# Feed-forward up product: every second tile pair as seven quarter products of 256 columns

## The chip, the cores and the metric

The kernel runs on one core of a Trainium2 chip. The metric is the time of one execution on the device in microseconds (us); shown are the median of the runs and, for a profiled execution, its own time.

## What is computed

The reference runs two blocks over 512 tokens of width 1024, in float32. The change touches one product of the first:

```python
h = _rmsnorm(x, g_pre_ffn[i])
u = _causal_dwconv(h @ w_up[i], w_conv[i], b_conv[i])
a, v = u[..., :D_FF], u[..., D_FF:]
x = x + _rmsnorm((jax.nn.gelu(a) * v) @ w_down[i], g_post_ffn[i])
```

`w_up` is 1024 x 5632: 22 gate tiles of 128 output features and 22 value tiles. The convolution is causal, of width 3, along the tokens.

## The kernel before

Instructions are written by hand for each engine, in the order in which that engine runs them; semaphores order the engines. Each float32 matrix of the large products is split in two of the rounded type fp32r, a high part (a rounded copy) and a low part (the rest), and a product is the sum of three: high weights by high x, high weights by low x, low weights by high x.

In the up product (the stage, 418 to 657.6 us) the weights are the stationary operand and x, transposed, the moving one: `hT_r` is its high part, `up_low` its low part, 8 blocks of 128 features by 512 tokens. For every tile `split_features` (L423) gives 16 matmuls at L431 as soon as the high part of the tile is there, and 8 at L434 when the low part is: 24 matmuls of 512 columns, and 48 for a pair of gate tile and value tile. The sums of a pair stand in two of the eight PSUM banks, `2 * (j % 4) + w`, so four pairs are in flight.

The other engines, for tile n of pair j:
- SP loads the 512 KB tile into one of 12 ring slots (L2102), up to 12 tiles ahead; the slot is free once PE has used the tile in it.
- ACT makes the high part (`high_act`, L379), one tile ahead and into one of two places, once PE has used the tile before the last; then it takes the finished tile through the last tap of the convolution with its bias (L2763), and once a pair applies gelu (L2770).
- POOL makes the low part (`low_pool`, L394), a subtraction of 1024 columns.
- DVE adds the other two taps from PSUM (L3065, L3067) and multiplies gate and value into `gT` (L3071). At the last pair it also splits the first two row tiles of the down product (L420, L421).

Other lines that the rows name: L456, a product with the tokens stationary, 416 and 280 columns wide, same type; L1165, a product in float32; L421 and L2719, other splits; L2311, the transposed x going to SBUF ahead of the stage; L1256, expert weights; L724, L3085 and L2970, other elementwise work. The down product (L476) follows the stage.

## Time and profile before

| | us |
|---|---|
| median of 3 runs | 1539.93 (1539.74 to 1540.53) |
| profiled execution, its own time | 1538.59 |
| its span | 1536.8 |
| the stage, pairs 0 to 21 | 418 to 657.6 |
| share of the span: PE, DVE, ACT, POOL busy | 97%, 43%, 33%, 33% |

The span runs from the first to the last instruction on record; 1.8 us lie around it. A busy PE share of 97% says that TensorE almost always had a matmul in it, and not that every matmul was needed. Matmuls overlap, so what one costs is the distance of two starts.

### The profile page before, as it was taken

Reading aid. Unit: us, or ns where it says so; the run is one execution under the profiler, and the core shown is the slowest. Engines: PE = TensorE matmul, PEld = TensorE weight load, DVE = VectorE, ACT = ScalarE, POOL = GpSimd, SP = SyncE. Lnnn points to the kernel's source line nnn. Section 1 sums busy time; section 2 is a strip of 40 time slices with the busy share of each in tenths; the row PEclk is TensorE's granted clock in tenths of the full one; section 3 lists DMA queues with packets and bytes.
Section 4 is the critical chain, followed back from the end, with each engine's and each line's share of the span. In section 5 each row is a group of like instructions: output and inputs, shape, how many; then the busy total and the mean of one; then the engine's idle time right before and its main releaser. Section 6 shows DMA issues by size and latency. Waiting matters only on the chain.

```text
span 1536.8 us, 19531 instructions
## 1 busy us (share of the span) xinstructions
PE 1495.9 (97%) x7629; PEld 1019.5 (66%) x7630; DVE 667.6 (43%) x1141; ACT 508.5 (33%) x917; POOL 513.6 (33%) x328
## 2 busy tenths in 40 slices
PE   8999999999999999999999999999999999999997
PEld 7976677888788888888888777468543443433433
DVE  4157664224733333423335778664533232332334
ACT  4246664223533333321246333424111111111112
POOL 3454664445344444444724362622100010010000
PEclk9999999999999999999999999999999999999999
DMA  8233002322322222232323222267999999999996
GB/s 313 98 109 95 1 2 97 98 100 99 115 96 96 96 96 96 97 97 99 97 92 122 91 82 69 109 256 289 361 429 428 431 418 430 429 429 421 424 426 252
DMA packets 52636, 306.87 MB, mean 200 GB/s; under 512 B 7098, under 2 KB 7354, under 8 KB 40001
## 3 DMA queue, kind: packets, MB, share of 16 engines
q1 hardware_dynamic: 47872, 292.03, 49.2%
q0 software_dynamic: 4096, 11.49, 2.0%
q10 hardware_dynamic: 576, 2.10, 0.3%
q8 instruction: 63, 1.03, 0.3%
q14 instruction: 29, 0.23, 0.1%
HBM read 303.39 MB, written 4.19 MB: 200 GB/s over the span
## 4 chain that ended last, share of the span: by engine, by line
PE 86%; DMA 6%; DVE 5%; ACT 1%; POOL 1%; issue 1%; SPq 0%; DVEq 0%; ACTq 0%
PE banks L431 19%; PE banks L1256 13%; PE banks L476 12%; PE banks L434 9%; DMA ring<-experts 6%; PE banks L1302 5%; PE banks L1311 3%; PE banks L1056 2%; PE banks L456 2%; PE banks L2484 2%; PE banks L2468 2%; PE banks L2550 1%; PE banks L2454 1%; PE banks L914 1%; PE banks L915 1%; PE banks L2443 1%
## 5 line engine op out<-in xcount | busy, mean ns | idle before, releaser
L394 POOL TENSOR_TENSOR arena_r<-ring,arena_r 128x1024 fp32r<-128x1024 f32 x143 | 353.2, 2475 | 414.1 <-ACT arena_r L379 394.5
L379 ACT ACTIVATE arena_r<-ring 128x1024 fp32r<-128x1024 f32 x143 | 150.5, 1058 | 441.4 <-PE banks L434 279.4
L431 PE MATMUL banks<-hT_r,arena_r 128*128 128x512 f32 x640 | 250.0, 391 | 0.0
L431 PE MATMUL banks<-arena_r 128*128 128x512 f32 x640 | 249.1, 389 | 0.0
L1256 PE MATMUL banks<-ring,arena 128*64 128x512 f32 x704 | 222.5, 605 | 12.0 <-DMA ring<-experts 12.0
L476 PE MATMUL banks<-arena_r 128*128 128x512 f32 x784 | 183.5, 389 | 0.6 <-DVE arena_r L421 0.6
L476 PEld LDWEIGHTS banks<-arena_r 128*128 128x128 f32 x784 | 147.1, 188 | 31.5 <-POOL arena_r L394 1.0
L1256 PEld LDWEIGHTS banks<-ring,arena 128*64 128x64 f32 x704 | 70.5, 139 | 142.4 <-issue 141.5
L431 PEld LDWEIGHTS banks<-hT_r,arena_r 128*128 128x128 f32 x640 | 120.1, 188 | 29.0 <-issue 3.4
L431 PEld LDWEIGHTS banks<-arena_r 128*128 128x128 f32 x640 | 120.2, 188 | 25.1 <-issue 0.2
L751 POOL MEMSET arena<- 128x1024 f32 x15 | 14.3, 952 | 341.8 <-PE banks L1209 332.8
L434 PE MATMUL banks<-hT_r,arena_r 128*128 128x512 f32 x520 | 128.4, 389 | 0.0
L1949 DVE TENSOR_TENSOR resid<-resid,banks 128x1024 f32<-128x1024 f32 x60 | 70.6, 1218 | 127.2 <-PE banks L1311 127.2
L1302 PE MATMUL banks<-arena 128*64 128x512 f32 x496 | 113.6, 595 | 2.5 <-DMA arena<-experts 2.2
L1256 PE MATMUL banks<-arena 128*64 128x512 f32 x278 | 115.9, 595 | 0.0
L434 PEld LDWEIGHTS banks<-hT_r,arena_r 128*128 128x128 f32 x520 | 97.6, 188 | 20.3
L3065 DVE SCALAR_TENSOR_TENSOR arena<-banks,colt,arena 128x511 f32<-128x511 f32 x44 | 33.0, 750 | 151.8 <-ACT arena L2763 151.8
L1302 PEld LDWEIGHTS banks<-arena 128*64 128x64 f32 x496 | 36.5, 137 | 66.3 <-issue 60.5
L1311 PE MATMUL banks<-arena_r,colt_r 128*128 128x512 f32 x256 | 67.5, 404 | 0.1
L1518 ACT ACTIVATE arena<-banks 128x512 f32<-128x512 f32 x16 | 9.6, 597 | 165.6 <-PE banks L1268 165.6
L1311 PEld LDWEIGHTS banks<-arena_r,colt_r 128*128 128x128 f32 x256 | 45.5, 188 | 23.4 <-issue 14.6
L1938 DVE SCALAR_TENSOR_TENSOR arena_r<-banks,colt,arena_r 128x512 fp32r<-128x512 f32 x32 | 24.0, 751 | 82.2 <-ACT arena_r L1548 82.2
(506 smaller groups left out, 2171.6 us busy)
## 6 DMA issues: line engine op xcount, KB each, us to landing
ring<-stream SPq DMA_DIRECT2D x164, 512.0 KB, 3.3
arena<-experts SPq DMA_DIRECT2D x35, 2048.0 KB, 15.6
ring<-experts SPq DMA_DIRECT2D x32, 2048.0 KB, 16.6
ring<-experts SPq DMA_DIRECT2D x17, 1024.0 KB, 17.3
arena<-experts SPq DMA_DIRECT2D x31, 512.0 KB, 10.1
arena<-experts SPq DMA_DIRECT2D x11, 1024.0 KB, 15.9
ring<-experts SPq DMA_DIRECT2D x14, 512.0 KB, 6.4
hT<-experts SPq DMA_DIRECT2D x8, 512.0 KB, 11.0
```

What stands on the lines that cost most here:

```text
L379: nc.scalar.activation(parts(name, m)[:, 0, :], tile(tile_n), ACT.Copy).then_inc(S["w_high"], 1)
L394: nc.gpsimd.tensor_tensor(w[:, 1, :], tile(tile_n), plain(w[:, 0, :]), ALU.subtract).then_inc(S["w_low"], 1)
L431: nc.tensor.matmul(pb[:, bank, :], w[:, 0, k * P:(k + 1) * P], b[:, k, :], start=(k == 0 and part == 0), stop=False)
L434: last = nc.tensor.matmul(pb[:, bank, :], w[:, 1, k * P:(k + 1) * P], high[:, k, :], start=False, stop=(k == ND - 1))
L456: last = nc.tensor.matmul(pb[:, bank0 + i, 0:width], a[:, k, i * P:(i + 1) * P], w[:, v, q * width:(q + 1) * width], start=(k == 0 and par ...
L476: last = nc.tensor.matmul(pb[:, 2 * i + h, :], u[row], w[:, v, h * 512:(h + 1) * 512], start=(k == 0 and row + v == 0), stop=(k == K - 1 a ...
L1056: last = nc.tensor.matmul(pb[:, 2 * i + h, :], rows[row][:, i * P:(i + 1) * P], w[:, v, h * 512:(h + 1) * 512], start=(k == 0 and part == ...
L1256: last = nc.tensor.matmul(pb[r, bank, :], XT[:, k, r], weights(b, c + e, k * 512, (k + 1) * 512), start=(k == 0), stop=(k == ND - 1))
L1302: last = nc.tensor.matmul(pb[r, 3 + h, :], hbT[:, k, r], weights(b, 4 + e, at, at + 512), start=(k == 0), stop=(k == 3))
L1311: last = nc.tensor.matmul(pb[:, bank, :], spread_r[:, i * P:(i + 1) * P], y[:, h * 512:(h + 1) * 512], start=(part == 0), stop=(part == 1 ...
L1949: TT(half, half, pb[:, first:second + 1:second - first, :], ALU.add).then_inc(S["added"], 1)
L3065: L(nc.vector.scalar_tensor_tensor(out=c[:, 1:T], in0=u[:, 0:T - 1], scalar=col("w_conv", 2 * NF + m), in1=c[:, 1:T], op0=ALU.mult, op1=AL ...
```

## The change

Pairs 2, 4, ... 20 (ten, `MIXED`) are computed in another way, the twelve others as before. Take the pair's weights as 2 x 2 blocks, gate and value by the two halves of the 1024 features, and x as 2 x 2 blocks, the two halves of the features by the two halves of the tokens. Eight quarter products (128 outputs, 512 features, 256 tokens) make the pair; the change makes seven from sums of the blocks (Winograd's form) and joins them by additions:

- PE: `up_term`, seven products of 12 matmuls of 256 columns, 84 in place of 48 of 512. Term q writes half a bank of banks 4 to 7; plain pairs use banks 0 to 3, two in flight.
- DVE, once ahead of the stage's work: 4 sums `hT_r + up_low` of x quarters, t1 to t4 from them, and their low parts (`x_low`), all of 1024 columns. For each changed pair: `weight_sums`, 4 operations of 512 columns in SBUF, and `join`, 7 of 256 columns with a PSUM operand.
- ACT: the high parts of t1 to t4, and for each changed pair 7 copies of 512 columns (`term_high`) in place of 2 of 1024, and a copy of the first product (`take_first`). Their order is s3, s4, value_2, gate_1, gate_2, s2, s1 (`TERM_ORDER`), while PE takes gate_1 first.
- POOL: 7 subtractions of 512 columns in place of 2 of 1024, in the same order.
- SP: the t parts lie in eight of the twelve ring slots until the stage ends, so tiles from pair 2 on use four. A load now waits until the tile two pairs back is split. Eight of the down tiles are loaded at the stage's end.
- Some semaphores are shared under a new name (`gate_sig`, `branch_hi`, `branch_lo`), with counts to match.

```diff
+MIXED = range(2, NF, 2)
+PLAIN = [j for j in range(NF) if j not in MIXED]
+LIVE = 4
...
+TERMS = ["gate_1 x_1", "gate_2 x_2", "s2 t2", "s1 t1", "s3 t3", "s4 x_4", "value_2 t4"]
+TERM_ORDER = [4, 5, 6, 0, 1, 2, 3]
+NQ = len(TERMS)
...
+PLACES_OF = [(0, 0), (0, 1), (1, 0), (1, 1), (2, 0), (2, 1), (3, 0)]
...
+        quads = [(slice(4 * k, 4 * k + 4), slice(256 * t, 256 * t + 256)) for k in range(2) for t in range(2)]
+        h_quads = [x_sums[:, 4096 + 1024 * q:5120 + 1024 * q].rearrange("p (k t) -> p k t", k=4) for q in range(4)]
+        t_whole = {t: x_sums[:, 1024 * q:1024 * q + 1024].rearrange("p (k t) -> p k t", k=4) for q, t in enumerate(("t1", "t2", "t3", "t4"))}
+        t_parts = {t: [ring_r[:, spare_slots[at + v], :].rearrange("p (k t) -> p k t", k=4) for v in range(2)]
+                   for t, at in (("t1", 4), ("t2", 6), ("t3", 0), ("t4", 2))}
+        x_parts = [[part[:, k, tok] for part in (hT_r, up_low)] for k, tok in quads]
+        t_parts.update({"x_1": x_parts[0], "x_2": x_parts[2], "x_4": x_parts[3]})
+        term_home = [ar_r(2048, 1024), ar_r(3072, 1024), ar_r(0, 1024), ar_r(1024, 1024), ar_r(22528, 1024), ar_r(23552, 1024),
...
+            elif name == "up" and m // 2 - 1 in MIXED:
+                act.wait_ge(S["up_part"], terms_done(m // 2 - 1, 3 if m % 2 else 1))
...
+                before = max(other for other in range(n) if slot(other) == slot(n))
+                if n >= W_UP + 4 + LIVE and W_UP <= before < W_DOWN and slot(n) in live_slots:
+                    sp.wait_ge(S["w_low"], split_at(before - before % 2 + 1))
+                else:
+                    sp.wait_ge(S["w_used"], emptied_at(n))
...
-            low_pool(pool, "up", 2)
+            for j in range(1, NF):
+                if j in PLAIN:
+                    low_pool(pool, "up", 2 * j, 2 * j + 2)
+                    continue
+                for q in TERM_ORDER:
+                    high, low = term_parts[q][:, 0, :], term_parts[q][:, 1, :]
+                    pool.wait_ge(S["w_high"], term_made(j, q))
+                    nc.gpsimd.tensor_tensor(low, term_source(j, q), plain(high), ALU.subtract).then_inc(S["w_low"], 1)
...
+            def up_term(j, q):
+
+                weight, (high, low) = term_parts[q], t_parts[TERMS[q].split()[1]]
+                pe.wait_ge(S["w_high"], term_made(j, q))
+                for k in range(4):
+                    for part, src in enumerate((high, low)):
+                        nc.tensor.matmul(term_bank(j, q), weight[:, 0, k * P:(k + 1) * P], src[:, k, :], start=(k == 0 and part == 0), stop=False)
+                pe.wait_ge(S["w_low"], term_made(j, q))
+                for k in range(4):
+                    last = nc.tensor.matmul(term_bank(j, q), weight[:, 1, k * P:(k + 1) * P], high[:, k, :], start=False, stop=(k == 3))
+                return last
+
             for j in range(NF):
-                if j >= 4:
-
-                    pe.wait_ge(S["up_dve"], 2 * (j - 3))
-                for w in range(2):
-                    split_features(pe, "up", 2 * j + w, 2 * (j % 4) + w, hT_r, up_low, 2)
+                if j in PLAIN:
+                    if j >= 2:
+                        pe.wait_ge(S["up_dve"], 2 * PLAIN[PLAIN.index(j) - 2] + 2)
+                    for w in range(2):
+                        split_features(pe, "up", 2 * j + w, 2 * (PLAIN.index(j) % 2) + w, hT_r, up_low, 2)
+                    continue
+                if j > 2:
+                    pe.wait_ge(S["up_dve"], 2 * (j - 2) + 2)
+                for q in range(NQ - 1):
+                    if TERMS[q].split()[1] in ("t1", "t2", "t3"):
+                        pe.wait_ge(S["up_sums"], summed(TERMS[q].split()[1], "low"))
+                    up_term(j, q).then_inc(S["up_part"], 1)
+                pe.wait_ge(S["up_sums"], summed("t4", "low"))
+                up_term(j, NQ - 1).then_inc(used, 2)
...
+            def term_high(j, q):
+                if q < 4:
+                    act.wait_ge(S["w_used"], W_UP + 2 * (j - 1) + (1 if q < 2 else 2))
+                elif j == 2:
+                    act.wait_ge(S["w_used"], W_UP)
+                elif q < NQ - 1:
+                    act.wait_ge(S["up_part"], terms_done(j - 2, q))
+                else:
+                    act.wait_ge(S["w_used"], W_UP + 2 * (j - 2) + 2)
+                name = TERMS[q].split()[0]
+                if name in SUMS:
+                    act.wait_ge(S["up_sums"], summed(j, name))
+                else:
+                    arrived(act, W_UP + 2 * j + (name == "value_2"))
+                nc.scalar.activation(term_parts[q][:, 0, :], term_source(j, q), ACT.Copy).then_inc(S["w_high"], 1)
...
+            high_act(act, "up", 2)
+            conv_last(0, 0)
+            x_high("t1")
+            x_high("t2")
+            high_act(act, "up", 3)
+            conv_last(0, 1)
+            act.wait_ge(S["w_low"], made(W_UP + 1))
+            x_high("t3")
+            act.wait_ge(S["w_low"], made(W_UP + 3))
+            x_high("t4")
+            gelu(0)
+            for q in TERM_ORDER[:5]:
+                term_high(2, q)
+            conv_last(1, 0)
+            for j in MIXED:
+                for q in TERM_ORDER[5:]:
+                    term_high(j, q)
+                conv_last(j - 1, 1)
+                gelu(j - 1)
+                take_first(j)
+                for w in range(2):
+                    high_act(act, "up", 2 * j + 2 + w)
                 for w in range(2):
                     conv_last(j, w)
-                act.wait_ge(S["up_dve"], 2 * j + 1)
-                nc.scalar.activation(ga[:, j % 2, :], cva[:, j % 2, 0, :], ACT.Gelu_apprx_tanh).then_inc(S["up_gelu"], 1)
+                gelu(j)
+                if j + 2 in MIXED:
+                    for q in TERM_ORDER[:5]:
+                        term_high(j + 2, q)
+                else:
+                    high_act(act, "down", 0)
+                conv_last(j + 1, 0)
...
+            for q, (k, tok) in enumerate(quads):
+                ins = nc.vector.tensor_tensor(h_quads[q], plain(hT_r[:, k, tok]), plain(up_low[:, k, tok]), ALU.add)
+            L(ins)
+            nc.vector.tensor_tensor(t_whole["t1"], h_quads[1], h_quads[0], ALU.subtract).then_inc(summing, 1)
+            nc.vector.tensor_tensor(t_whole["t3"], h_quads[3], h_quads[1], ALU.subtract).then_inc(summing, 1)
+            dve.wait_ge(summing, summed("t1", "whole"))
+            nc.vector.tensor_tensor(t_whole["t2"], h_quads[3], t_whole["t1"], ALU.subtract).then_inc(summing, 1)
+            dve.wait_ge(summing, summed("t2", "whole"))
+            nc.vector.tensor_tensor(t_whole["t4"], h_quads[2], t_whole["t2"], ALU.subtract).then_inc(summing, 1)
+
+            def weight_sums(j):
+                gate_tile, value_tile = tile(W_UP + 2 * j), tile(W_UP + 2 * j + 1)
+                first, second = slice(0, 512), slice(512, 1024)
+                arrived(dve, W_UP + 2 * j)
+                arrived(dve, W_UP + 2 * j + 1)
+                if j > 2:
+                    dve.wait_ge(S["w_low"], term_made(j - 2, TERM_ORDER[-1]))
+                nc.vector.tensor_tensor(s_home["s1"], value_tile[:, first], value_tile[:, second], ALU.add).then_inc(summing, 1)
+                dve.wait_ge(summing, summed(j, "s1"))
+                nc.vector.tensor_tensor(s_home["s2"], s_home["s1"], gate_tile[:, first], ALU.subtract).then_inc(summing, 1)
+                nc.vector.tensor_tensor(value_tile[:, first], gate_tile[:, first], value_tile[:, first], ALU.subtract).then_inc(summing, 1)
+                dve.wait_ge(summing, summed(j, "s2"))
+                nc.vector.tensor_tensor(s_home["s4"], gate_tile[:, second], s_home["s2"], ALU.subtract).then_inc(summing, 1)
...
+                q, other, to = {"c11": (1, first_term, pb[:, 4, 0:256]), "u2": (2, first_term, second_sum),
+                                "u4": (3, second_sum, fourth_sum), "u3": (4, second_sum, third_sum), "c12": (5, fourth_sum, pb[:, 4, 256:512]),
+                                "c22": (3, third_sum, pb[:, 5, 256:512]), "c21": (6, third_sum, pb[:, 5, 0:256])}[what]
...
+            conv(0, 0)
+            x_low("t1")
+            x_low("t2")
+            weight_sums(2)
+            x_low("t3")
+            conv(0, 1)
+            gated_rows(0)
+            x_low("t4")
+            conv(1, 0)
+            for j in MIXED:
+                conv(j - 1, 1)
+                gated_rows(j - 1)
+                for what in ("c11", "u2", "u4", "u3", "c12", "c22", "c21"):
+                    join(j, what)
+                for w in range(2):
+                    conv(j, w)
+                gated_rows(j)
+                if j + 2 in MIXED:
+                    weight_sums(j + 2)
+                else:
+                    dve.wait_ge(S["up_g"], 2)
+                    dve.wait_ge(S["w_low"], term_made(j, TERM_ORDER[-1]))
+                    split_dve(dve, chain, "down", gT, 0, 2)
+                conv(j + 1, 0)
```

DVE, from the transposed x to the first gated product, before (`colt` holds the convolution's weights, `banks` is PSUM):

```order
L2311 SCALAR_TENSOR_TENSOR arena_r<-banks,colt,hT_r 128x512 [waits copied_act] x8
L3065 SCALAR_TENSOR_TENSOR arena<-banks,colt,arena 128x511 [waits up_conv]
L3067 SCALAR_TENSOR_TENSOR arena<-banks,colt,arena 128x510 [waits dve_chain]
L3065 SCALAR_TENSOR_TENSOR arena<-banks,colt,arena 128x511 [waits up_conv]
L3067 SCALAR_TENSOR_TENSOR arena<-banks,colt,arena 128x510 [waits dve_chain]
L3071 TENSOR_TENSOR arena<-arena 128x512 [waits up_gelu,up_dve]
```

From the same point in the changed kernel (`x_sums` holds the x quarters and t1 to t4, `ring` their parts and the loaded tiles):

```order
L2425 SCALAR_TENSOR_TENSOR arena_r<-banks,colt,hT_r 128x512 [waits copied_act] x8
L3253 TENSOR_TENSOR x_sums<-hT_r,arena_r 128x1024 [waits hT_low]
L3253 TENSOR_TENSOR x_sums<-hT_r,arena_r 128x1024 x3
L3255 TENSOR_TENSOR x_sums<-x_sums 128x1024 [waits dve_chain]
L3256 TENSOR_TENSOR x_sums<-x_sums 128x1024
L3258 TENSOR_TENSOR x_sums<-x_sums 128x1024 [waits up_sums]
L3260 TENSOR_TENSOR x_sums<-x_sums 128x1024 [waits up_sums]
L3286 SCALAR_TENSOR_TENSOR arena<-banks,colt,arena 128x511 [waits up_conv]
L3288 SCALAR_TENSOR_TENSOR arena<-banks,colt,arena 128x510 [waits dve_chain]
L3279 TENSOR_TENSOR ring_r<-x_sums,ring_r 128x1024 [waits h_high] x2
L3269 TENSOR_TENSOR arena<-ring 128x512 [waits w_landed5,w_landed4]
L3271 TENSOR_TENSOR arena<-arena,ring 128x512 [waits up_sums]
```

Eight sums now stand ahead of the first convolution, and two low parts and the weight sums of pair 2 ahead of the second.

DVE in the changed kernel from the last join of pair 2 to the sums of pair 4:

```order
L3310 TENSOR_TENSOR banks<-junk,banks 128x256 [waits up_sums,w_used]
L3286 SCALAR_TENSOR_TENSOR arena<-banks,colt,arena 128x511 [waits up_conv]
L3288 SCALAR_TENSOR_TENSOR arena<-banks,colt,arena 128x510 [waits dve_chain]
L3286 SCALAR_TENSOR_TENSOR arena<-banks,colt,arena 128x511 [waits up_conv]
L3288 SCALAR_TENSOR_TENSOR arena<-banks,colt,arena 128x510 [waits dve_chain]
L3294 TENSOR_TENSOR arena<-arena 128x512 [waits up_gelu,up_dve]
L3269 TENSOR_TENSOR arena<-ring 128x512 [waits w_low,w_landed5,w_landed4]
L3271 TENSOR_TENSOR arena<-arena,ring 128x512 [waits up_sums]
L3272 TENSOR_TENSOR ring<-ring 128x512
L3274 TENSOR_TENSOR arena<-ring,arena 128x512 [waits up_sums]
```

The weight sums of a pair stand behind the joins, convolutions and gated product of the changed pair before it.

ACT in the changed kernel over the first pairs:

```order
L482 ACTIVATE arena_r<-ring 128x1024 [waits w_used,w_landed10]
L2899 ACTIVATE arena<-banks,colt 128x512 [waits w_used]
L2908 ACTIVATE ring_r<-x_sums 128x1024 [waits up_sums] x2
L482 ACTIVATE arena_r<-ring 128x1024 [waits w_used,w_landed11]
L2899 ACTIVATE arena<-banks,colt 128x512 [waits w_used]
L2908 ACTIVATE ring_r<-x_sums 128x1024 [waits up_sums,w_low] x2
L2904 ACT_TABLE_LOAD
L2904 ACTIVATE arena<-arena 128x512 [waits up_dve]
L2924 ACTIVATE arena_r<-ring 128x512 [waits up_sums,w_used]
L2924 ACTIVATE arena_r<-arena 128x512 [waits up_sums,w_used]
L2924 ACTIVATE fifth_home_r<-ring 128x512 [waits w_landed5,w_used]
L2924 ACTIVATE arena_r<-ring 128x512 [waits w_landed4,w_used] x2
```

The high part of tile 3 (the second row of L482) now stands behind the copies of t1 and t2, and the five first copies for pair 2 behind the gelu of pair 0. Before, it was L379, L2763, L379, L2763, gelu.

## Rows read from the trace of the kernel before

**Rows 1.** The page: span, busy time by engine, one DMA issue (count, KB, us).
```profile
span 1536.8 us, 19531 instructions
...
PE 1495.9 (97%) x7629; PEld 1019.5 (66%) x7630; DVE 667.6 (43%) x1141; ACT 508.5 (33%) x917; POOL 513.6 (33%) x328
...
ring<-stream SPq DMA_DIRECT2D x164, 512.0 KB, 3.3
```
**Rows 2.** Busy time by stretch: us, PE, PEld, DVE, ACT, POOL, clock, DMA.
```profile
440.00:657.60 217.60, 217.60 (x961) 180.18 (x961) 77.32 (x104) 79.44 (x100) 96.14 (x40) 1.00 0.29 97
```
**Rows 3.** The chain in order of time: start us, us, what.
```profile
423.67 3.63 PE banks L431 x16
427.30 1.81 PE banks L434 x8
```
**Rows 4.** PE in order of time: the third pair's first matmul.
```profile
439.83 0.39 PE L431 MATMUL banks<-hT_r,arena_r 128*128 128x512 f32 x1
```
**Rows 5.** Line 456 alone, by stretch: us, PE, PEld, clock, DMA.
```profile
57.10:75.15 18.05, 18.05 (x96) 17.93 (x96) 1.00 0.36 117
75.15:87.50 12.35, 12.35 (x97) 12.27 (x96) 1.00 0.38 128
```
**Rows 6.** PEld in order of time, the shortest full loads.
```profile
1075.65 2.98 PEld L1165 LDWEIGHTS banks<-arena,resid 128*128 128x128 f32 x26 [0.15 <-DVE arena L1872]
```
**Rows 7.** Groups by line and shape: busy us, mean ns, idle before.
```profile
L394 POOL TENSOR_TENSOR arena_r<-ring,arena_r 128x1024 fp32r<-128x1024 f32 x143 | 353.2, 2475 | 414.1 <-ACT arena_r L379 394.5 <-DVE arena L1699 19.2
...
L724 POOL TENSOR_TENSOR arena<-arena 128x512 f32<-128x512 f32 x4 | 5.1, 1272 | 0.0
...
L379 ACT ACTIVATE arena_r<-ring 128x1024 fp32r<-128x1024 f32 x143 | 150.5, 1058 | 441.4 <-PE banks L434 279.4 <-PE banks L476 99.6 <-PE banks L2555 24.8
...
L2719 ACT ACTIVATE arena_r<-hT 128x512 fp32r<-128x512 f32 x8 | 4.4, 616 | 0.0
...
L2763 ACT ACTIVATE arena<-banks,colt 128x512 f32<-128x512 f32 x44 | 33.5, 761 | 0.0
...
L3085 DVE TENSOR_TENSOR arena<-arena 128x1024 f32<-128x1024 f32 x3 | 3.7, 1225 | 2.6 <-ACT arena L2791 2.6
...
L3065 DVE SCALAR_TENSOR_TENSOR arena<-banks,colt,arena 128x511 f32<-128x511 f32 x44 | 33.0, 750 | 151.8 <-ACT arena L2763 151.8
...
L2970 DVE COPY arena<-banks 128x256 f32<-128x256 f32 x12 | 4.9, 408 | 1.1 <-PE banks L2468 1.1
```
**Rows 8.** DVE and POOL in order of time, where both subtract.
```profile
378.06 13.72 DVE L421 TENSOR_TENSOR arena_r<-arena,arena_r 128x512 fp32r<-128x512 f32 x5 [2.90 <-ACT arena_r L410]
...
377.59 16.45 POOL L394 TENSOR_TENSOR arena_r<-ring,arena_r 128x1024 fp32r<-128x1024 f32 x6 [4.29 <-ACT arena_r L379]
...
647.95 2.41 POOL L394 TENSOR_TENSOR arena_r<-ring,arena_r 128x1024 fp32r<-128x1024 f32 x1 [3.04 <-ACT arena_r L379]
...
650.14 0.77 DVE L3071 TENSOR_TENSOR arena<-arena 128x512 f32<-128x512 f32 x1
```
**Rows 9.** In order of time, before and in the first pairs.
```profile
417.71 4.69 DVE L2311 SCALAR_TENSOR_TENSOR arena_r<-banks,colt,hT_r 128x512 fp32r<-128x512 f32 x7
...
432.98 0.69 DVE L3071 TENSOR_TENSOR arena<-arena 128x512 f32<-128x512 f32 x1 [0.48 <-ACT arena L2770]
...
424.91 2.39 POOL L394 TENSOR_TENSOR arena_r<-ring,arena_r 128x1024 fp32r<-128x1024 f32 x1 [10.26 <-ACT arena_r L379]
...
430.95 1.28 ACT L2770 ACT_TABLE_LOAD   x1
```
**Rows 10.** PE in order of time, two restarts after an idle stretch.
```profile
249.56 0.50 PE L442 MATMUL banks<-arena_r 128*128 128x512 f32 x1 [0.54 <-DVE hT_r L3029]
...
1190.36 1.11 PE L1256 MATMUL banks<-ring,arena 128*64 128x512 f32 x2 [3.23 <-DMA ring<-experts]
```
**Rows 11.** Busy time by stretch around the second restart, columns as in 2.
```profile
1188.00:1192.00 4.00, 1.64 (x4) 0.61 (x6) 0.64 (x1) 0.00 (x0) 0.00 (x0) 0.80 1.02 434
1192.00:1196.00 4.00, 4.00 (x18) 1.58 (x16) 0.00 (x0) 0.00 (x0) 0.00 (x0) 0.77 0.99 422
```

More of the change, by code:

```diff
@@ L89, with loads_before, emptied_at @@
          "inverse": (21, 8, W_IDFT, 2)}
+MIXED = range(2, NF, 2)
+PLAIN = [j for j in range(NF) if j not in MIXED]
+LIVE = 4
 def slot(n):
+    if W_UP + 4 <= n < W_DOWN:
+        return (W_DOWN + (n - W_DOWN) % LIVE - W_OUT2) % RING
     return (n - W_OUT2) % RING
+def loads_before(n):
+    return sum(slot(other) == slot(n) for other in range(n))
+def emptied_at(n):
+    before = max(other for other in range(n) if slot(other) == slot(n))
+    if n >= W_DOWN + LIVE and before < W_DOWN:
+        return W_DOWN
+    return before + 1
 def landings(s):
@@ L2771, in _ @@
+            high_act(act, "down", 1)
+            conv_last(NF - 1, 1)
+            gelu(NF - 1)
             nc.scalar.activation(st[:, 449:450], cs("eps"), ACT.Sqrt)
```

185 lines of the change are left out of this document (129 added, 56 removed).

## The prediction

> **What bounds the kernel now.** The page comes first: a span of 1536.8 us, TensorE busy for 1495.9 of them, no other engine above 43% [rows 1]. Then the stage of the change, by stretch: from the third pair on, 440.0 to 657.6, PE is busy for all of its 217.6 us at full granted clock, while DVE, ACT and POOL work 77, 79 and 96 us of it [rows 2]. The chain in order of time says what a tile costs: 16 matmuls in 3.63 us and 8 in 1.81, so 5.44 us for 24 of 512 columns, **226.7 ns each** [rows 3]. That is the distance between starts; the 389 ns printed beside one matmul [rows 4] includes its way through the array and must not be summed. A pair is 10.88 us. The stage is bound by matmul issue and by nothing else: a saved matmul is saved time, if the other three engines keep up with what replaces it.
>
> **What PE saves.** In ten pairs (2, 4, ... 20) 48 matmuls of 512 columns (10.88 us) become 84 of 256: seven products of 12. The price of one is not in this trace: no product of that shape (128 by 128 weights, rounded type, 256 columns, a load for each) stands in it. The nearest are line 456's, in the same type: 416 columns, 18.05 us for 96, 188.0 ns; 280 columns, 12.35 us for 96, 128.6 ns [rows 5]. The slope, 0.437 ns a column, gives 118 ns at 256; the overhead seen at 512 (226.7 less 512 columns at 2.4 GHz, 13.4) gives 120. I take **119 ns**, since 280 is only 24 columns away. Upper bound: 128.6, if the distance doesn't fall any further because the weight loads set it. Lower bound: 26 loads of 128 by 128 follow each other in 2.98 us, (2.98 - 0.19) / 25 = 112 ns [rows 6]. At 119 a changed pair takes 84 x 0.119 = 10.00 us and saves 0.88; ten save **8.9 us** (0.8 at 128.6, 14.7 at 112).
>
> The Trainium skill has another price. Its page "TensorE: Matmul & The Clock Gate", section "Back-to-back issue gap", gives columns / 2.4 + 2.5 ns, so 109 ns here, and 216 at 512, where this trace has 226.7. By the page alone ten pairs would save 10 x (48 x 0.2158 - 84 x 0.1092) = 12 us. I go by the rows.
>
> **What the others gain in work, steady state.** Durations [rows 7]: POOL subtraction 1.27 us for 512 columns (2.40 for 1024), ACT copy 0.62 (1.06), ACT's convolution step 0.76, DVE step 0.75, DVE over 1024 SBUF columns 1.22, over 256 of PSUM 0.41; over 512 of SBUF 0.69 [rows 9]. Per two pairs (20.9 us): POOL 7 x 1.27 + 2 x 2.40 = 13.7; DVE 4 weight sums, 7 joins, 8 steps, 2 products, 13; ACT 7 short and 2 long copies, 4 convolution steps, 2 gelu and the saved quarter, about 11. All fit. What decides is one chain that now closes a loop. The weight sums of pair j+2 stand on DVE behind the joins, the convolution and the gated product of pair j, because DVE works in order; and PE's first product of j+2 needs four ACT copies and four POOL subtractions, though only the fourth is its own (order s3, s4, value_2, gate_1). Let E be the end of pair j on PE. Last join done E + 0.6; two convolutions on DVE, 4 x 0.78, to E + 3.6; gated product to 4.3; s1, s2, s3 to 6.3; ACT's copy of s3 to 6.9; POOL, 3 x 1.23 + 1.27, to **E + 12.0**. (1.23 apart, an estimate: the next one begins a little before the end of the last, as on DVE, where seven steps of 0.75 take 4.69 [rows 9].) PE needs it at E + 10.88 (the plain pair) + 8 x 0.119 = **E + 11.83**. That is a stall of 0.3 us with semaphores, and a restart after a stall costs 0.1: the first matmul after one lasts 0.50 instead of 0.39 [rows 10]. Nine pairs at 0.4: **3.6 us**. The later products don't wait: POOL delivers every 1.23 us, PE takes 1.43.
>
> **The entry into pair 2.** PE reaches it at 439.83 [rows 4]. DVE gets free at 417.71 + 4.69 = 422.4 [rows 9] and then has, in order: 4 sums of x quarters and 4 t sums of 1024 columns (8 x 1.15, with the same overlap), one convolution (1.55), two low parts (2.3), s1 to s3 (2.0). That is 15.0 us, to 437.4, even undisturbed. But DVE and POOL get in each other's way. Where both subtract in SBUF, five DVE operations of 0.69 us took 13.72 us, while six of POOL's took 16.45, 2.74 each [rows 8]: each waits for the other's whole operation. The smaller pair of rows shows one collision: POOL ends at 650.36, and the DVE product begun at 650.14 ends 0.55 later [rows 8]. DVE steps with a PSUM operand keep 750 ns [rows 7]. So the subtraction of tile 2, at 424.9 before [rows 9], holds up the fourth x sum by 2.1 us, and that of tile 3 the low part of t1 by 1.8. s3 is ready at 422.4 + 19.0 = 441.4. Four ACT copies later, 443.8, PE may start: **4.1 us late**. Its second half needs four POOL subtractions, which begin at 442.2 and meet on DVE the low part of t3 (to 443.2), the first gated product and the low part of t4 (1.1 us more): ready at 449.4 where PE would go on at 445.0, **4.5 us more**. Together 8.6 us, and nothing gives them back, since the stage is bound by PE. ACT is no help: the copy of tile 3 stands in its queue behind the copies of t1 and t2, and the table load of 1.28 us [rows 9] behind the t copies.
>
> **The clock.** PE stood idle for 3.23 us before 1190.36 [rows 10], and the next two stretches of 4 us have a granted clock of 0.80 and 0.77 [rows 11]: part of them at 1.2 instead of 2.4 GHz, (0.20 + 0.23) x 4 = 1.7 us of full-speed work lost. Two idle stretches of 4.1 and 4.5 us with 1 us of work between should do the same once where PE is working: **1.7 us** (0 to 3.4).
>
> **What costs nothing.** In the stage only four ring slots are live; a load waits for the split of the tile two pairs back, some 9 us before its own sums, and lands in 3.3 [rows 1]. After the stage eight down tiles are loaded at once, with four there, 4 x 5.44 us of cover. The last pair is plain, as before, so the passage into the down product is the same. The queue of SP holds nothing else there. The renamed semaphores do nothing.
>
> **Sum.** -8.9 + 8.6 + 3.6 + 1.7 = **+5.0 us**. The profiled execution's own time is 1538.59, so 1543.6; the median of the runs shown is 1539.93, 1.3 above it, so **1544.9 us**.
>
> **Rivals.**
> - *Pair 2 is entered almost in time; faster.* If DVE and POOL share better than [rows 8], the entry costs 2.7 us (undisturbed sum above, ACT and POOL behind it), with no fall of the clock. -8.9 + 2.7 + 3.6 = -2.6: **1537.3**. It decides from 3 us of entry stall downwards. Against it: both durations in [rows 8]. For it: the subtractions seen there are all of 1024 columns, and most of POOL's in the entry are of 512.
> - *The matmul is shorter, 112 ns* [rows 6]. It saves 5.8 more, but PE then reaches each second half earlier (8 x 0.007) and waits for it longer, so some 5.3 of it remain: -0.3, **1539.6**. The 109 ns of the Trainium skill (same page and section) points this way; the 226.7 ns of this trace at 512 columns do not.
> - *The loop is slower*: 0.1 us more at each of the six hand-overs between engines makes 1 us a pair in place of 0.4: +10.4, **1550.3**. For it: one chain runs through PE, DVE, ACT, DVE, ACT and POOL with no slack left, so whatever I left out lengthens it.
> - *The matmul stays at 128.6 ns* [rows 5]: 8.1 less saved, and stalls 0.08 us a pair smaller: +12.4, **1552.3**.
>
> **How the numbers follow.** No change and the edit can be told apart beyond about 0.2%, 3.1 us, so below 1536.8 is faster and above 1543.0 slower. Chances: forecast 0.45, entry in time 0.18, shorter matmul 0.12, slower loop 0.17, longer matmul 0.08. The forecast's own width, 2 us either way, puts a fifth of it within 0.2%; the entry in time is above 1536.8 half the time; the shorter matmul lies mostly inside; the last two are slower. Faster 0.18, same 0.27, slower 0.55. The range goes from the entry in time with a slightly better matmul, 1535.5, to the slower loop and most of the longer matmul, 1551.5.
>
> **What would show it.** Right: starts of the new matmuls 119 ns apart; PE idle before the third pair for about 4 us at 440, waiting for ACT, and 4.5 us inside its first product, waiting for POOL; DVE sums of 2 to 3 us instead of 1.2 between 425 and 448; a granted clock below 1.0 there and nowhere else in the stage; 0.3 to 0.5 us idle before the fifth, seventh ... pair's first low product, ended by POOL. Wrong: matmuls at 112 or 128 ns, an idle of under 3 us at the third pair, or stalls that wait for a load or for DVE's joins.

## The result: 0.24% slower, and the profile after

The changed kernel takes 1544.53 us (median of 10 runs, 1541.54 to 1546.76) beside 1540.3 for the kernel before: ratio 1.0024, 95% interval 1.0015 to 1.0034, or 3.7 us slower (2.3 to 5.2). Executed again (experiment 10, with its own runs of the kernel before beside it) it took 1546.22, ratio 1.0040 (1.0027 to 1.0053), or 6.2 us slower (4.2 to 8.2). The page of the first profile, in which `split_features` is now at L534 and L537, the quarter products at L2692 (high weights) and L2695 (low weights):

```profile
span 1542.2 us, 20400 instructions
...
PE 1495.0 (97%) x7989; PEld 1031.8 (67%) x7990; DVE 746.6 (48%) x1263; ACT 537.1 (35%) x981; POOL 560.5 (36%) x378
...
PE 76%; DVE 10%; DMA 7%; POOL 4%; ACT 2%; issue 1%; SPq 0%; ACTq 0%; DVEq 0%
```

The last line gives the shares of the chain that ended last. In the kernel before it was:

```profile
PE 86%; DMA 6%; DVE 5%; ACT 1%; POOL 1%; issue 1%; SPq 0%; DVEq 0%; ACTq 0%
```

PE's busy time over the whole kernel is the same as before [rows 1], though 8 us of matmuls are gone. In the stage it is 2.0 us less (237.65 against 239.66): part of the matmuls ran at half the clock, and the length printed for the last one before a wait covers some of the wait. Ahead of the stage it is 1.6 us more, at a lower granted clock near 110 us (last section). More of the chain passes through DVE and POOL than before. By stretch (columns as in [rows 2]), the entry into pair 2 and what follows:

```profile
440.00:444.00 4.00, 2.74 (x13) 1.93 (x11) 3.97 (x6) 2.77 (x4) 0.00 (x0) 1.00 0.00 0
444.00:448.00 4.00, 2.00 (x8) 1.78 (x8) 3.93 (x5) 4.00 (x8) 3.62 (x3) 0.70 0.00 0
448.00:452.00 4.00, 0.45 (x2) 0.37 (x2) 3.96 (x5) 0.91 (x3) 4.00 (x3) 0.50 0.00 0
452.00:456.00 4.00, 4.00 (x21) 4.00 (x21) 2.61 (x4) 1.12 (x3) 3.74 (x3) 0.52 0.00 0
456.00:460.00 4.00, 4.00 (x36) 4.00 (x35) 1.20 (x3) 1.84 (x2) 2.64 (x2) 1.00 0.72 266
```

From 444 to 452 PE is busy for 2.45 of 8 us, while DVE hardly stops, and PE's granted clock falls from 2.4 to 1.2 GHz (0.70, then 0.50); from 452 to 456 PE works without a break, still at half the clock. PE in order of time, there and in pair 4:

```profile
440.76 1.98 PE L537 MATMUL banks<-hT_r,arena_r 128*128 128x512 f32 x8
446.00 0.58 PE L2692 MATMUL banks<-hT_r,arena_r 128*128 128x256 f32 x1 [3.26 <-ACT arena_r L2924]
...
447.66 0.41 PE L2692 MATMUL banks<-arena_r 128*128 128x256 f32 x1
451.63 1.22 PE L2695 MATMUL banks<-hT_r,arena_r 128*128 128x256 f32 x4 [3.55 <-POOL arena_r L2283]
...
474.42 0.28 PE L2692 MATMUL banks<-arena_r 128*128 128x256 f32 x1
474.76 0.74 PE L2695 MATMUL banks<-hT_r,arena_r 128*128 128x256 f32 x4
...
476.78 1.12 PE L2692 MATMUL banks<-ring_r,arena_r 128*128 128x256 f32 x8
477.74 0.64 PE L2695 MATMUL banks<-ring_r,arena_r 128*128 128x256 f32 x4
478.22 1.12 PE L2692 MATMUL banks<-ring_r,arena_r 128*128 128x256 f32 x8
```

The last three lines give the price: 8 matmuls from 476.78 to 477.74, 4 to 478.22, **120 ns each**. Before the first low product of pair 4 the distance is 474.76 - 474.42 = 0.34 us instead of 0.12. The chain in order of time names its cause, four POOL subtractions in a row behind one ACT copy:

```profile
468.93 0.64 ACT arena_r L2924
469.58 0.07 issue
469.64 2.55 POOL arena_r L2283 x2
472.20 1.25 POOL fifth_home_r L2283
473.45 1.26 POOL arena_r L2283
```

Why pair 2 was late is seen on DVE and POOL in order of time (L3253: x sums; L3279: low parts of t1 to t4; L3272: s3; L3294: gated product):

```profile
424.55 6.83 DVE L3253 TENSOR_TENSOR x_sums<-hT_r,arena_r 128x1024 f32<-128x1024 f32 x4
431.42 1.23 DVE L3255 TENSOR_TENSOR x_sums<-x_sums 128x1024 f32<-128x1024 f32 x1
...
437.53 4.12 DVE L3279 TENSOR_TENSOR ring_r<-x_sums,ring_r 128x1024 fp32r<-128x1024 f32 x2
...
442.90 0.68 DVE L3272 TENSOR_TENSOR ring<-ring 128x512 f32<-128x512 f32 x1
...
446.80 1.45 DVE L3294 TENSOR_TENSOR arena<-arena 128x512 f32<-128x512 f32 x1
448.17 2.28 DVE L3279 TENSOR_TENSOR ring_r<-x_sums,ring_r 128x1024 fp32r<-128x1024 f32 x1
```

```profile
427.04 3.26 POOL L497 TENSOR_TENSOR arena_r<-ring,arena_r 128x1024 fp32r<-128x1024 f32 x1 [10.26 <-ACT arena_r L482]
437.03 2.41 POOL L497 TENSOR_TENSOR arena_r<-ring,arena_r 128x1024 fp32r<-128x1024 f32 x1 [6.73 <-ACT arena_r L482]
444.38 2.07 POOL L2283 TENSOR_TENSOR arena_r<-ring,arena_r 128x512 fp32r<-128x512 f32 x1 [4.95 <-ACT arena_r L2924]
446.42 1.28 POOL L2283 TENSOR_TENSOR arena_r<-arena,arena_r 128x512 fp32r<-128x512 f32 x1
447.66 1.71 POOL L2283 TENSOR_TENSOR fifth_home_r<-ring,fifth_home_r 128x512 fp32r<-128x512 f32 x1
```

Four x sums take 6.83 instead of some 4.7 us while POOL splits tile 2; two low parts take 4.12 instead of 2.35 beside tile 3. POOL's own operations grow too, 2.07 and 1.71 instead of 1.27. This is the mutual blocking of [rows 8]. ACT was not what held up the start: it stood idle for 1.20 us, waiting for s3, before its first copy for pair 2.

**Where the time is.** The profiles are compared by the starts of PE's matmuls. This profile enters the stage 2.12 us later than before's, with the same instructions ahead of it (experiment 8 and the last section show that the kernel before does so as well), so the stage is compared by itself: 5.7 us longer, from its first to its last matmul. Pair 2 starts 4.06 us late and takes 16.67 us instead of the 10.08 of 84 matmuls; the nine later changed pairs take 10.39 each, the plain ones 10.91. The stage's 5.7 us lie above the interval of the time (2.3 to 5.2), those of experiment 10, 6.0, inside its own; the last section comes back to this.

### The profile page after: what moved, and what is told of

The parts are those of the page before. It is cut to its first block, busy times and chain, and to the rows that moved or that the text cites. A ratio compares the mean times of both kernels' runs of the same rounds, so it can differ in the third digit from the quotient of the medians.

```text
span 1542.2 us, 20400 instructions
## 1 busy us (share of the span) xinstructions
PE 1495.0 (97%) x7989; PEld 1031.8 (67%) x7990; DVE 746.6 (48%) x1263; ACT 537.1 (35%) x981; POOL 560.5 (36%) x378
## 4 chain that ended last, share of the span: by engine, by line
PE 76%; DVE 10%; DMA 7%; POOL 4%; ACT 2%; issue 1%; SPq 0%; ACTq 0%; DVEq 0%
PE banks L1359 13%; PE banks L579 12%; PE banks L534 9%; DMA ring<-experts 7%; PE banks L1405 5%; PE banks L537 5%; PE banks L2692 4%; POOL arena_r L2283 3%; PE banks L1414 3%; PE banks L2695 2%; PE banks L559 2%; PE banks L2598 2%; PE banks L1159 2%; PE banks L2582 2%; PE banks L2664 1%; PE banks L2568 1%
## 5 line engine op out<-in xcount | busy, mean ns | idle before, releaser
L497 POOL TENSOR_TENSOR arena_r<-ring,arena_r 128x1024 fp32r<-128x1024 f32 x123 | 309.7, 2526 | 300.5 <-ACT arena_r L482 281.1
L482 ACT ACTIVATE arena_r<-ring 128x1024 fp32r<-128x1024 f32 x123 | 129.2, 1058 | 317.3 <-PE banks L537 138.3
L534 PE MATMUL banks<-hT_r,arena_r 128*128 128x512 f32 x480 | 188.0, 392 | 0.3 <-ACT arena_r L482 0.3
L534 PE MATMUL banks<-arena_r 128*128 128x512 f32 x480 | 187.0, 390 | 0.0
L579 PE MATMUL banks<-arena_r 128*128 128x512 f32 x784 | 183.5, 389 | 0.6 <-DVE arena_r L524 0.6
L579 PEld LDWEIGHTS banks<-arena_r 128*128 128x128 f32 x784 | 147.1, 188 | 31.5 <-POOL arena_r L497 1.0
L534 PEld LDWEIGHTS banks<-hT_r,arena_r 128*128 128x128 f32 x480 | 90.1, 188 | 23.2 <-issue 3.4
L534 PEld LDWEIGHTS banks<-arena_r 128*128 128x128 f32 x480 | 90.2, 188 | 18.6 <-issue 0.2
L537 PE MATMUL banks<-hT_r,arena_r 128*128 128x512 f32 x360 | 88.9, 389 | 0.0
L537 PEld LDWEIGHTS banks<-hT_r,arena_r 128*128 128x128 f32 x360 | 67.6, 188 | 14.0
L2283 POOL TENSOR_TENSOR arena_r<-ring,arena_r 128x512 fp32r<-128x512 f32 x30 | 40.2, 1353 | 70.8 <-ACT arena_r L2924 70.8
```

The costliest lines, as they stand in the source:

```text
L482: nc.scalar.activation(parts(name, m)[:, 0, :], tile(tile_n), ACT.Copy).then_inc(S["w_high"], 1)
L497: nc.gpsimd.tensor_tensor(w[:, 1, :], tile(tile_n), plain(w[:, 0, :]), ALU.subtract).then_inc(S["w_low"], 1)
L534: nc.tensor.matmul(pb[:, bank, :], w[:, 0, k * P:(k + 1) * P], b[:, k, :], start=(k == 0 and part == 0), stop=False)
L537: last = nc.tensor.matmul(pb[:, bank, :], w[:, 1, k * P:(k + 1) * P], high[:, k, :], start=False, stop=(k == ND - 1))
L579: last = nc.tensor.matmul(pb[:, 2 * i + h, :], u[row], w[:, v, h * 512:(h + 1) * 512], start=(k == 0 and row + v == 0), stop=(k == K - 1 a ...
L2283: nc.gpsimd.tensor_tensor(low, term_source(j, q), plain(high), ALU.subtract).then_inc(S["w_low"], 1)
```

## The experiments

Each is the changed kernel with one edit, unless it says otherwise. The second column is the time against the kernel before as executed beside it, from the ratio and its interval; the third the stage in the profile, against before's 239.6 us.

| | time, us (95%) | stage, us |
|---|---|---|
| changed kernel | +3.7 (2.3 to 5.2) | +5.7 |
| 1 price on PE alone | -9.4 (-11.6 to -7.4) | -7.8 |
| 2 gate_1 split first | +0.5 (-0.8 to 1.8) | +2.7 |
| 3 filler in the waits | +4.6 (3.2 to 6.0) | +3.9 |
| 4 POOL shortened, tiles 2, 3 | +0.8 (-0.5 to 2.2) | +2.3 |
| 5 first changed pair is 4 | -1.1 (-2.5 to 0.3) | -0.5 |
| 6 terms without sums ahead | -4.2 (-5.9 to -2.5) | -2.5 |
| 7 both, and banks | -6.2 (-8.3 to -4.2) | -5.3 |
| 9 weight sums first | +2.8 (1.2 to 4.3) | +2.7 |
| 10 changed kernel again | +6.2 (4.2 to 8.2) | +6.0 |
| 11 filler again | +4.8 (2.9 to 6.5) | +4.0 |

**1, the price of the matmuls.** In the kernel before, for pairs 2, 4, ... 20:

```diff
+                    for i in range(28):
+                        half, k, part = i % 2, i // 4, i // 2 % 2
+                        nc.tensor.matmul(pb[:, bank, 256 * half:256 * half + 256], weight[:, 0, k * P:(k + 1) * P],
+                                         (hT_r, up_low)[part][:, k, 256 * half:256 * half + 256], start=(i == 0), stop=False)
```

and 14 more on the low part.

> The kernel before, in which PE alone is changed: in pairs 2, 4, ... 20 it issues 84 matmuls of 256 columns (42 a tile, 28 on the high part and 14 on the low part) in place of 48 of 512. The last quarter of the sums of those pairs is left out; the other engines do what they did. Theory: the price is the distance of two starts seen in the changed kernel, 0.120 us, so a pair takes 10.08 instead of 10.88 and the whole saving reaches the end: 10 x 0.80 = 8.0 us, about 1532.3 against 1540.3. Rival 1: something else in the stage (ACT's copy, a ring slot, a load) takes the place of PE as the bound and gives part of it back: 0 to -5 us, with waits of PE inside the short pairs. Rival 2: the distance is shorter when two neighbours share their weights, down to 0.109: -17 us at most.

Measured: 1528.65 us, ratio 0.9939. The chain of the first changed pair:

```profile
439.96 3.35 PE banks L2585 x28
443.31 1.68 PE banks L2590 x14
444.99 3.36 PE banks L2585 x28
448.35 1.68 PE banks L2590 x14
450.03 3.65 PE banks L431 x16
```

3.35 / 28 and 1.68 / 14 are 120 ns, though four in a row use the same weights; the pair takes 10.07 us and waits for nothing. The stage is 7.8 us shorter, 8.0 expected. The median fell by more, 11.6 us (9.4 by the ratio, whose interval holds the 8.0). The stage bears out the theory, and both rivals fall: PE waits nowhere in the short pairs, and the distance is not below 120 ns. The gain of the matmuls alone is 8 us, and the changed kernel gives back 13.5 (5.7 + 7.8 in the stage).

**2, the order of the terms.**

```diff
-TERM_ORDER = [4, 5, 6, 0, 1, 2, 3]
+TERM_ORDER = [0, 1, 4, 5, 6, 2, 3]
```

> The changed kernel with one line edited: ACT and POOL split the terms in the order gate_1, gate_2, s3, s4, value_2, s2, s1, so that what PE needs first comes first and does not stand behind the weight sums. Theory (the stall in each later pair is POOL's fourth place behind DVE's sums): the nine gaps of about 0.25 us before the first low product vanish, -2.0 to -2.4; in pair 2 the first two products start almost in time, and the long wait moves to the third product (s2): its first half about 0.8 us late, its second half 4 to 5 us, again for POOL. Together 1.5 to 2 us less there. In all 4.3 us below the changed kernel, about 1540.0. Rival (the loop is set by the sums themselves, wherever the copies stand): gaps of 0.2 us or more reappear before s2's or s3's low product in every changed pair, and the time stays within 1 us of the changed kernel.

Measured: 1540.02 us, ratio 1.0003. All nine later pairs take 10.07 us with no gap, so the rival falls. In pair 2 the wait moved to the third product, as expected:

```profile
445.56 1.18 PE L2692 MATMUL banks<-ring_r,arena_r 128*128 128x256 f32 x8 [0.64 <-ACT arena_r L2924]
451.53 1.22 PE L2695 MATMUL banks<-ring_r,arena_r 128*128 128x256 f32 x4 [4.78 <-POOL arena_r L2283]
```

The stage lost 3.0 of its 5.7 us (4.3 expected), nearly all of it in the later pairs. At the entry little was won: pair 2 starts 1.1 us late instead of 4.06, but takes 19.44 us instead of 16.67. The long wait is there, and the clock still fell behind it, later than before (0.76 from 448, 0.50 from 452, 0.89 from 456 to 460), so that the slow time lies almost wholly in PE's work.

**9, the same stall from the other end.** This edit shortens the chain on DVE and leaves the order of the terms:

```diff
+                if j + 2 in MIXED:
+                    weight_sums(j + 2)
                 for w in range(2):
                     conv(j, w)
                 gated_rows(j)
```

> The changed kernel in which DVE makes the weight sums of pair j + 2 right behind the joins of pair j, ahead of pair j's convolution and gated product, instead of behind them; the order of the terms and the entry into pair 2 stay. Theory (the later stalls are the end of one chain: joins, convolution, gated product, sums, copies, subtractions): s3's copy on ACT now waits only for gelu, at the pair's end + 4.9 us instead of + 6.3, the fourth subtraction ends 1.4 us earlier and the nine gaps of 0.25 us before the first low product go; the entry stays as it is. The stage gets 2.2 us shorter, the time 2.2 us less than the changed kernel's. Rival (the stall is POOL's: seven subtractions, whenever the sums come): the gaps stay at 0.2 us or more.

Measured: 1542.32 us. The gaps are gone, every later changed pair takes 10.07, and the entry is as in the changed kernel (3.62 and 3.97 us between starts). The stage is 3.0 us shorter than the changed kernel's, 2.9 of it 9 x 0.32: a gap costs 0.32, since the matmul behind it starts slowly as well. Experiments 2 and 9 remove the stall by different links of one chain, so it is the chain, and the rival (POOL's seven subtractions as such) falls.

**4, who made DVE late.**

```diff
+                        nc.gpsimd.tensor_tensor(w[:, 1, 0:16], tile(W_UP + m)[:, 0:16], plain(w[:, 0, 0:16]), ALU.subtract).then_inc(S["w_low"], 1)
```

> The changed kernel in which POOL subtracts 16 columns instead of 1024 for tiles 2 and 3 (pair 1): the low part of these two tiles is left out but for 16 columns. Theory (DVE and POOL can't both work on two SBUF operands at once): the fourth x sum and the low part of t1 on DVE lose their 2.1 and 1.8 us of waiting, s3 is ready almost 4 us earlier, PE starts pair 2 in time (the gap of 3.65 us before it is under 0.5); the second gap, 4 to 4.5 us inside the first product, stays, since POOL's four subtractions still meet DVE's sums. In all 3.5 to 4.5 us below the changed kernel, about 1540.3. Rival (DVE was late for its own work or for ACT's copies, not for POOL): DVE's eight sums still take over 10 us in all, the gap before pair 2 stays above 3 us, and the time changes by less than 0.5 us.

Measured: 1540.57 us, ratio 1.0005. DVE and POOL in order of time:

```profile
426.20 4.66 DVE L3259 TENSOR_TENSOR x_sums<-hT_r,arena_r 128x1024 f32<-128x1024 f32 x4
...
437.00 2.35 DVE L3285 TENSOR_TENSOR ring_r<-x_sums,ring_r 128x1024 fp32r<-128x1024 f32 x2
```

```profile
428.65 1.13 POOL L2281 TENSOR_TENSOR arena_r<-ring,arena_r 128x16 fp32r<-128x16 f32 x1 [10.23 <-ACT arena_r L482]
436.51 0.22 POOL L2281 TENSOR_TENSOR arena_r<-ring,arena_r 128x16 fp32r<-128x16 f32 x1 [6.73 <-ACT arena_r L482]
```

6.83 became 4.66 and 4.12 became 2.35: 3.94 us given back, against 2.1 + 1.8 forecast. PE starts pair 2 only 0.1 us late; the second gap stayed (4.70 between starts), and the stage is 3.4 us shorter, just under the 3.5 to 4.5 forecast. POOL's 16 columns take 0.22 us alone and 1.13 beside DVE's x sums, so each side waits for the other. The rival falls. The Trainium skill says it so (page "SBUF — State Buffer", section "Terms"): the port pair of DVE and GpSimd is locked for a whole instruction, and the loser blocks; these lines agree.

**3 and 11, the clock.**

```diff
+            def filler(count):
+                for _ in range(count):
+                    nc.tensor.matmul(pb[:, 7, 256:512], hT_r[:, 0, 0:P], hT_r[:, 0, 0:256], start=True, stop=True)
```

> The changed kernel with matmuls that do nothing useful put where PE waits in pair 2: 27 of 256 columns before its first product (3.24 of 3.65 us) and 30 before the first low product (3.60 of 3.97 us), into half a bank that nobody reads. Theory: the clock fell because PE stood idle, so the granted clock stays near 1.0 between 440 and 460, matmuls keep a distance of 0.120, and the time falls by 1.3 to 1.7 us, to about 1542.9. Rival: the fall has another cause (the engines beside it, or it was chance): the clock falls all the same and the time is that of the changed kernel or up to 1 us more.

Measured: 1544.16 us. By stretch, columns as before:

```profile
444.00:448.00 4.00, 3.96 (x33) 3.76 (x32) 3.93 (x5) 4.00 (x8) 4.00 (x3) 1.00 0.00 0
448.00:452.00 4.00, 3.13 (x26) 2.93 (x25) 3.95 (x4) 0.85 (x2) 4.00 (x3) 1.00 0.02 4
```

The clock stayed up and the stage was 1.8 us shorter than the changed kernel's, but the time did not show it: the median moved by 0.4, and against the kernel before it is +4.6, where the changed kernel had +3.7. Hence a repetition, with the changed kernel beside it.

> The changed kernel once more, unchanged: a second profile of it and more executions, beside the next kernel. Theory: the stage is again 5.5 to 6 us longer than before's, with the same two long gaps and a granted clock that falls behind them; the time is 3.5 to 5 us above the kernel before. Rival: the fall of the clock in pair 2 was chance of one execution: granted clock 1.00 from 440 to 460 in this profile, and a stage 1.7 us shorter than in the first.

> The changed kernel with the 57 idle matmuls in PE's two waits of pair 2, once more: in the first look the clock stayed at 1.00 there and the stage was 1.9 us shorter, but the median of the executions had not moved. Theory: the clock falls there in every execution of the changed kernel and never with the filler, so the time is 1.5 to 2 us below the changed kernel in the same call. Rival: it falls in some executions only, or the clock kept here falls elsewhere: the difference of the medians is below 0.8 us.

Measured: 1546.22 (5 runs) and 1543.71 us (6 runs), 2.5 us apart. In the second profile of the changed kernel the clock fell again (0.50 from 448 to 456); with the filler it is 1.00. The stages are 2.0 us apart, those of the first pair of profiles 1.8. The other profiles say the same. In the five without filler in which PE's longest wait at the entry was 3.6 to 4.8 us (the changed kernel twice, experiments 2, 4 and 9) the granted clock fell there to 0.50; in the two with filler (3, 11) and the three in which the longest wait was 0.7 to 1.75 us (5, 6, 7) it stayed at 1.00. So the idleness of PE as the cause of this fall, and 1.8 to 2.0 us as its price in the stage, are shown. In the times the gain is not shown: the ratios give +6.2 and +4.8 us with intervals that overlap, and +3.7 and +4.6 the first time, the other way round.

**5, a later start.** `MIXED = range(4, NF, 2)`, with pairs 2 and 3 plain in each engine's list.

> The changed kernel with the first changed pair at 4 instead of 2 (nine changed pairs; the order of the terms stays). Theory: what cost 8 us at the entry was only that PE came too soon; 21.8 us later DVE has long made its sums. Nine pairs at 48 x 0.2267 - 84 x 0.120 = 0.80 save 7.2 us; against that 0.25 us in each changed pair (2.3), 0.8 more in the first, some 2 us where the third and fifth tile pairs wait for ACT's late copies and for a bank (now two in flight), and no fall of the clock. In all -2 us against the kernel before, between -3 and -0.5: about 1538.3. Rival (the sums and the copies of x disturb the stage wherever they stand): PE still idle for 3 us or more ahead of or inside the first changed pair, the clock falls, and the time is above the kernel before.

Measured: 1538.27 us, ratio 0.9993, which can't be told from no change. The first changed pair takes 11.58 us instead of 16.67 and starts without delay, the clock stays at 1.00, eight pairs keep their 10.39. The 1.5 us that the first changed pair takes beyond 10.07 are one wait for POOL. The wait for a bank before the third tile pair is there too (1.94 us between two starts, 1.55 of them idle, ended by DVE's convolution). The forecast was -2 us, between -3 and -0.5; -1.1 by the ratio and -0.5 in the stage are at its near end. The rival falls: the sums disturb only who needs them soon.

**6, what needs no sum goes ahead.**

```diff
-TERM_ORDER = [4, 5, 6, 0, 1, 2, 3]
+TERM_ORDER = [0, 1, 6, 2, 3, 4, 5]
...
-                for q in TERM_ORDER[5:]:
+                for q in TERM_ORDER[3:]:
```

> The changed kernel with the terms split in the order gate_1, gate_2, value_2, s2, s1, s3, s4 (two lines), the first three ahead of the last step of the pair before, the other four behind it: the terms in which no sum of DVE is needed come first, and s2, the third product, is POOL's fourth subtraction of its pair but its first that waits for DVE. Theory: no gap in the later pairs (s2 is split at the end of the plain pair + 1.9 us, needed at + 3.8), and at the entry the third product waits 2 to 2.5 us in place of 5. Against the kernel before -8.0 + 4.5 for the entry, with 0 to 1.7 for the clock: -3.5 to -1.8, about 1537.6. Rival (whoever waits for the end of the plain pair becomes late): gaps before the third product's halves in every changed pair, 0.3 us or more each, and a time of 1540 or above.

Measured: 1535.96 us, ratio 0.9973 (0.9962 to 0.9984): **faster than before** with ten changed pairs. Later pairs take 10.07 us, with no gap before the third product, so the rival falls. The entry costs 5.3 us against 4.5 forecast: pair 2 starts 1.1 us late and takes 14.25 us, with three waits for POOL in it, the longest (1.75 us) in the third product. The clock stays at 1.00.

**7, all of it.** Experiments 5 and 6 together, and the third and fourth tile pair in banks 4 to 7.

> Both together and the banks: changed pairs 4, 6, ... 20, the terms split in the order gate_1, gate_2, value_2, s2, s1, s3, s4, and the third and fourth tile pair in banks 4 to 7, so that they don't wait for the convolution of the first two. Theory: nothing is left of the three costs: 9 x 0.80 = 7.2 us saved, 0.3 to 1 us of small waits while DVE and ACT make the sums of x, no fall of the clock: -6.5 us against the kernel before, about 1533.8, ratio 0.9958. Rival (the mixing costs something of its own in every pair, whichever the order): changed pairs longer than 10.2 us, or the plain ones longer than 10.9, and the time above 1537.

Measured: 1533.04 us (1531.22 to 1535.43), ratio 0.9960 (0.9946 to 0.9973): 6.2 us faster than the kernel before and some 10 faster than the change. All nine changed pairs take 10.07 us and start without delay, so the rival falls. The waits of PE in the stage are one for DVE's transposed x at its start, as in the kernel before, and two for ACT's copy, which stands behind those of t1 to t4:

```profile
PE banks L534 <- ACT arena_r L482: 1.1, 2, 0.7
PE banks L545 <- DVE arena_r L2425: 0.9, 1, 0.9
```

From the start of the second tile pair to that of the third it is 12.45 us instead of 10.88: 1.6 us, where 0.3 to 1 was forecast.

**8, the kernel before, a second profile.**

> The kernel before, unchanged, for a second profile of it. The changed kernel and four variants reach the stage 0 to 3.8 us later than the profile of before does, by steps at about 110 us where all have the same instructions, and lose 1.6 us some 60 us behind the stage, the variant of the kernel before among them. Theory: both are chance of the single executions: this profile has its stage of the same 239.6 us, but its start may be 0 to 4 us off, and some 1.6 us of waiting behind the stage are gone. Rival: the profiles of before agree within 0.3 us everywhere, and the late start is the changed kernel's.

Measured: 1538.9 us. The stage is 239.6 us again, entered 1.66 us later than in the first profile, and 1.6 us are gone again behind it, at 1024 to 1032 (not some 60 us behind the stage, as the expectation has it). There the first profile of before has a granted clock of 0.82 and 0.75, and all 12 others have 1.00. Both differences come without any change of the kernel, and the rival falls. The stretches that differ, in the first profile of before, in this one and in experiment 10:

```profile
108.00:112.00 4.00, 4.00 (x48) 3.11 (x47) 1.49 (x3) 1.59 (x3) 0.89 (x1) 1.00 0.00 0
112.00:116.00 4.00, 4.00 (x11) 1.74 (x10) 3.93 (x3) 3.07 (x5) 4.00 (x4) 1.00 0.00 0
```

```profile
108.00:112.00 4.00, 4.00 (x45) 3.13 (x44) 1.57 (x3) 1.67 (x3) 0.96 (x1) 0.84 0.00 0
112.00:116.00 4.00, 4.00 (x8) 1.55 (x7) 3.93 (x3) 1.47 (x3) 4.00 (x4) 0.73 0.00 0
```

```profile
108.00:112.00 4.00, 4.00 (x43) 3.50 (x42) 0.75 (x2) 0.82 (x2) 0.11 (x1) 0.67 0.00 0
112.00:116.00 4.00, 4.00 (x6) 1.69 (x5) 3.90 (x4) 1.96 (x4) 4.00 (x3) 0.50 0.00 0
```

## Why the prediction was right, point by point

1544.9 us was forecast, 1544.5 and 1546.2 were measured. Against the kernel before, 5.0 us more was forecast, and 3.7 (2.3 to 5.2) and 6.2 (4.2 to 8.2) were measured. The two profiles are 5.7 and 6.0 us longer in the stage.

| term | forecast | measured | from |
|---|---|---|---|
| PE, ten pairs | -8.9 | -8.0 | 10 x (10.88 - 84 x 0.120); experiment 1: -7.8 |
| late start of pair 2 | +4.1 | +4.06 | PE in order of time; 3.94 of it DVE's waiting for POOL, experiment 4 |
| inside its first product | +4.5 | +4.8 | pair 2 in experiments 3 and 11, 14.90 and 14.93, less 10.08 |
| clock | +1.7 | +1.8 to 2.0 | pair 2 with and without filler: 16.67 and 16.90 less those |
| nine stalls | +3.6 | +2.9 | 9 x (10.39 - 10.07); experiments 2 and 9 |
| sum | +5.0 | +5.6 to 5.8 | |

- *What PE saves.* The step "I take 119 ns" was mis-sized by 1 ns, which is 0.9 us over 840 matmuls. The overhead seen at 512 columns gave 120, the slope through 416 and 280 gave 118; the first was right. The Trainium skill's 109 ns (page "TensorE: Matmul & The Clock Gate", section "Back-to-back issue gap") is given there for a matmul by itself, and the section says that in a stream of weight loads and matmuls the spacing is set by both. The prediction's "by the page alone" took it for the price of such a stream; measured here are 120 ns.
- *What the others gain in work, steady state.* The chain is the one named, through joins, convolution, gated product, sums, copy and four subtractions: experiments 2 and 9 break it in two places. Its times hold too: with E at 462.68 (pair 2), the copy of s3 ends at E + 6.9 and the fourth subtraction at E + 12.0, both as forecast. The stall was forecast at 0.4 and is 0.32: PE's gap is 0.22 and the restart 0.1; POOL's subtractions are 1.25 us apart (starts at 469.64 and, three later, at 473.39), 1.23 forecast.
- *The entry.* Both halves hold to 0.3 us, and so does the cause of the first, by experiment 4. Counted from a stage that starts 2.12 us later, s3 is ready at 441.5 (441.4 forecast), pair 2 starts at 443.9 (443.8) and its second half at 449.5 (449.4). That POOL meets DVE in the second half as well is seen (2.07, 1.71, 2.28, 1.45 us) but no run removed it alone.
- *The clock.* It fell where forecast and by as much; the filler shows that the waits caused it.
- *What costs nothing.* No wait of PE for a load or a join appears in the stage. The passage into the down product cost nothing.
- *The rivals and the chances.* An entry in time would have needed POOL's 512-column operations to block less: they block all the same. Matmuls of 112 or 128.6 ns and a loop stall of 1 us did not occur. The three chances for faster, same and slower don't follow from those of the forecast and its rivals: four fifths of 0.45, with 0.17 and 0.08, make 0.61 slower and not 0.55.
- *Right for a reason that needs care.* The errors of the terms (0.9 of PE, 0.7 of the stalls) have opposite signs in the sum, and the time of executions scatters by 5 us (1541.54 to 1546.76) for reasons that the prediction did not have (below). The forecast of the stage was 0.7 to 1.0 us short; that the first median came within 0.4 us, between differences of 3.7 and 6.2, is partly luck.

## What to carry to other kernels

Where one engine bounds a stage, price what is removed there, and then look for the first moment at which the new helper work must be ready: here 8 us of saving were lost to an entry 4 + 4.8 us late, with 1.8 to 2.0 us for the clock and 2.9 for the stalls behind it, and the repair was to let PE start with what needs no preparation (order of the copies) and to begin two pairs later, not to make any operation faster. A new operation on DVE with two SBUF inputs is to be costed together with every GpSimd operation that it can meet, the whole length of each. In a loop, follow one chain round through all engines: the stall of 0.32 us went away by either of two edits in the order, with no work removed.
